# Feed-forward of a two-layer fp32 encoder step: another spread of the token scale, another order at its beginning, turn and end

## The reference, cut to what matters

```python
D_MODEL, D_FF, EPS = 1024, 4096, 1e-6

def rmsnorm(x, g):
    y = x * lax.rsqrt(jnp.mean(x * x, axis=-1, keepdims=True) + EPS)
    return y * g

def sq_relu_ffn(x, g, w1, w2):            # w1 (1024, 4096), w2 (4096, 1024), all float32
    h = jax.nn.relu(rmsnorm(x, g) @ w1)
    return (h * h) @ w2

for l in range(2):
    x = x + mixer[l](rmsnorm(x, norm_mix_g[l]))
    x = x + sq_relu_ffn(x, norm_ffn_g[l], w_ff1[l], w_ff2[l])
y = rmsnorm(x, norm_out_g)                # and the new caches and states
```

## Time and profile before

| | us |
|---|---|
| median of 3 runs (lowest, highest) | 2695.02 (2692.13, 2702.24) |
| the profiled execution | 2700.55 |
| its span, first to last instruction | 2698.6 |
| outside the span (the difference) | 1.95 |
| PE busy | 2607.2 (97%) |
| DVE, ACT, POOL busy | 1741.4, 957.2, 1499.1 |

### The profile page before, as it was taken

One profiled execution on the slowest core, in us unless ns is written; L12 is line 12 of the kernel. 1 busy time (PEld: TensorE's weight loads), 2 busy tenths in 40 slices (PEclk: granted clock), 3 DMA queues, 4 the chain that ended last, 5 costly groups with the idle time before them and its releaser, 6 DMA issues. The chain is left out here.

```text
span 2698.6 us, 44221 instructions
## 1 busy us (share of the span) xinstructions
PE 2607.2 (97%) x17409; PEld 2525.2 (94%) x17409; DVE 1741.4 (65%) x2291; ACT 957.2 (35%) x1828; POOL 1499.1 (56%) x1527
## 2 busy tenths in 40 slices
PE   7999999999998999999999999989999999899998
PEld 7998789999997999999989898979999999899997
DVE  5216956766666777778646464654766666777776
ACT  4112634333333434441413323142433333344444
POOL 6543523666665888873222321342466667688784
PEclk9999999999998999999999999999999999999999
DMA  6321021333345434432233241433133334534332
GB/s 196 71 55 42 2 113 66 119 141 140 140 149 196 152 138 141 140 130 74 37 98 42 76 83 55 97 115 131 50 139 140 140 140 178 199 135 144 136 134 95
DMA packets 161789, 308.21 MB, mean 114 GB/s; under 512 B 61628, under 2 KB 76988, under 8 KB 160816
## 3 DMA queue, kind: packets, MB, share of 16 engines
q1 hardware_dynamic: 86656, 243.19, 26.6%
q10 hardware_dynamic: 74656, 61.22, 7.8%
q0 software_dynamic: 272, 0.98, 0.1%
HBM read 204.18 MB, written 95.85 MB: 111 GB/s over the span
## 5 line engine op out<-in xcount | busy, mean ns | idle before, releaser
L741 POOL TENSOR_TENSOR w_lo<-w_raw,w_hi 128x256 fp32r<-128x256 f32 (+1 forms) x478 | 435.2, 923 | 267.4 <-ACT w_hi L2317 267.2
L1006 PE MATMUL psum<-a_hi,w_hi 128*128 128x288 f32 x2032 | 441.2, 299 | 12.1 <-DVE low L1760 11.7
L1760 DVE TENSOR_TENSOR low<-low,psum 128x576 f32<-128x576 f32 x441 | 330.7, 751 | 170.4 <-PE psum L1006 168.0
L1006 PE MATMUL psum<-a_lo,w_hi 128*128 128x288 f32 x2032 | 438.1, 298 | 0.0
L1006 PE MATMUL psum<-a_hi,w_lo 128*128 128x288 f32 x2032 | 437.8, 297 | 0.0
L2317 ACT ACTIVATE w_hi<-w_raw 128x256 fp32r<-128x256 f32 (+1 forms) x478 | 209.5, 456 | 537.8 <-POOL w_raw L755 305.0
L1006 PE MATMUL psum<-op_h,w_hi 128*128 128x288 f32 x2040 | 357.4, 297 | 16.3 <-DVE low L1760 13.8
L1006 PEld LDWEIGHTS psum<-a_hi,w_hi 128*128 128x128 f32 x2032 | 331.5, 191 | 14.4 <-DVE low L1760 12.7
L1006 PEld LDWEIGHTS psum<-a_lo,w_hi 128*128 128x128 f32 x2032 | 330.9, 191 | 0.0
L1006 PEld LDWEIGHTS psum<-a_hi,w_lo 128*128 128x128 f32 x2032 | 330.3, 190 | 0.0
L951 PE MATMUL psum<-a_hi,w_hi 128*128 128x384 f32 x1272 | 302.6, 346 | 17.8 <-DVE a_lo L1551 16.4
(11 more groups left out here) (314 smaller groups left out, 4623.9 us busy)
## 6 DMA issues: line engine op xcount, KB each, us to landing
w_raw<-in_wall SPq DMA_DIRECT2D x159, 512.0 KB, 4.5
ffn_rows<-low SPq DMA_DIRECT2D x224, 288.0 KB, 2.1
mid<-ffn_rows SPq DMA_DIRECT2D x52, 576.0 KB, 3.6
rbc<-ffn_rows SPq DMA_DIRECT2D x50, 576.0 KB, 3.7
mid<-in_wall SPq DMA_DIRECT2D x32, 512.0 KB, 4.5
low<-in_x ACTq DMA_DIRECT2D x16, 576.0 KB, 8.3
high<-in_mem_in ACTq DMA_DIRECT2D x32, 257.0 KB, 4.3
out_mem_s<-high ACTq DMA_DIRECT2D x32, 257.0 KB, 3.2
```

The costliest lines, as they stand in the source:

```text
L741: nc.gpsimd.tensor_tensor(w_lo_flat[:, at], src, w_hi_flat[:, at].bitcast(F32), ALU.subtract)\
L1006: r = mm(psum[:, bank + i, 0:QT], v[:, at.start + P * k:at.start + P * (k + 1)], rows(part, k)[:, qtok(i)], start=start and k == 0 and n == 0,
L1760: V.tensor_tensor(dst, dst, two(bank), ALU.add).then_inc(dn_read, 1)
```

## The change

It touches the three stretches of each feed-forward that were just described, and has three parts.

**First pair.** The diagonal on DVE goes. PE makes each half of the spread with six matmuls of 96 columns: the stationary operand is a column of `rstd12` repeated 128 times, the moving one the 96x96 identity. Both halves stand behind product 4. ACT loads its table for the root with a one-column Sqrt at the start of the feed-forward, and raises T3 later in its queue; DVE makes T1's low part ahead of the T4 difference, and has some low parts in another order.

**Turn.** Chunk 0's last row is staged in H0 instead of mid. DVE has the lowering of rows 4, 5, 6 of chunk 0 behind the adds 0, 2, 3 of unit 0, the last pair's last sum and ReLU behind add 4, and its other sums behind the products 6, 7, 8. SP reads rows (0,6) and (1,1) and the weights of unit 2 ahead of the last pair's last writes. Chunk 1's rows are raised and lowered at the products that two tables give: the raising at q = 10, 12, 16, 18, 22, 24, 27 (before: 5, 8, 11, ... 23), the lowering of one half each behind the adds 11 to 14, 17 to 20, 23 to 26, 28 and 29 (before: 7, 8, 10, 11, 13, 14, ... 25, 26).

**End.** `rest` and `add_squares` of the last chunk work on 576 columns in twice as many steps; in feed-forward 0 the rests of tiles 4 to 7 (before: 6 and 7) stand behind the last add.

```diff
+CHUNK0_AT = ("A", "A", "H0", "H1", "mid", "A", "H0")
+CHUNK1_HIGH = {10: 0, 12: 1, 16: 2, 18: 3, 22: 4, 24: 5, 27: 6}
+CHUNK1_LOW = {11: (0, 0), 12: (0, 1), 13: (1, 0), 14: (1, 1), 17: (2, 0), 18: (2, 1), 19: (3, 0), 20: (3, 1),
+              23: (4, 0), 24: (4, 1), 25: (5, 0), 26: (5, 1), 28: (6, 0), 29: (6, 1)}
...
-                per = {"A": 3, "mid": 26, "H0": 1, "H1": 1}[n]
+                per = {"A": 3, "mid": 25, "H0": 2, "H1": 1}[n]
...
                         sp.wait_ge(c_relu, 4 * PAIRS * (f + 1))
+                    elif q == 1:
+                        sp.wait_ge(d_lo, 14 * FC * f + 10)
                     else:
                         sp.wait_ge(d_lo, 14 * FC * f + 14 + 2 * (q - 1))
...
+                    if p == PAIRS - 1:
+                        sp.wait_ge(d_lo, 14 * FC * f + 6)
+                        rows_in(0, 6)
+                        next_rows(1, 1)
+                        sp.wait_ge(f_split, n0 + NPU + 7)
+                        down_load(2)
                     sp.wait_ge(t_out, 4 * n + 1)
                     keep(p, "T1")
                     if p == PAIRS - 1:
-                        sp.wait_ge(d_lo, 14 * FC * f + 10)
-                        rows_in(0, 6)
                         next_rows(1, 0)
-                        sp.wait_ge(f_split, n0 + NPU + 7)
-                        down_load(2)
                         sp.wait_ge(h_sq, 4 * n + 4)
                         keep(p, "B21")
...
-                for k in range(3):
-                    x_return(k)
+                x_return(0)
+                x_return(1)
                 for d in range(DUNITS):
                     c, j = divmod(d, 4)
-                    if d == 1:
+                    if d == 2:
+                        sp.wait_ge(t4_out, 16 * PAIRS * (f + 1))
+                        x_return(2)
                         sp.wait_ge(d_lo, 14 * FC * f + 12)
                         x_return(3)
                     if c + 1 < FC:
-                        for i in range(max(2 * j, d == 0), min(2 * j + 2, 7)):
+                        for i in range(2 if d == 0 else 2 * j, min(2 * j + 2, 7)):
...
-                    pe.wait_ge(diagonal, 2 * f + h + 1)
-                    if h:
-                        pe.wait_ge(rstd_copied, 2 * f + 1)
-                    for i in range(2):
-                        r = mm(psum[:, bank + i, 0:QT], ones[0:COLT, :], c21[0:COLT, qtok(i)], start=True, stop=True)
+                    pe.wait_ge(ff_sum, f + 1)
+                    for n in range(NC // 2):
+                        at = COLT * (n % 3)
+                        r = mm(psum[:, bank + n // 3, at:at + COLT],
+                               rstd12[0:COLT, NC // 2 * h + n:NC // 2 * h + n + 1].to_broadcast([COLT, P]),
+                               ident[0:COLT, 0:COLT], start=True, stop=True)
                     r.then_inc(rstd_done, 1)
...
                     product(Z, at, kt, rows, True, True, ready)
-                    if first:
-                        spread_scale(0, W)
                     at, kt, rows, ready = begin(4)
                     pe.wait_ge(up_read, r0 + 4 * p + 1)
                     product(X, at, kt, rows, False, False, ready)
                     if first:
-                        spread_scale(1, W)
+                        spread_scale(0, W)
+                        pe.wait_ge(up_read, r0 + 2)
+                        spread_scale(1, Z)
                     at, kt, rows, ready = begin(5)
                     product(V, at, kt, rows, True, True, ready)
                     at, kt, rows, ready = begin(6)
...
-                def scale_diagonal(h):
-
-                    n = NC // 2
-                    V.tensor_tensor(c21[0:COLT, :].rearrange("p (a b) -> p a b", a=n),
-                                    ident[0:COLT, 0:COLT].unsqueeze(1).to_broadcast([COLT, n, COLT]),
-                                    rstd12[0:COLT, n * h:n * (h + 1)].unsqueeze(2).to_broadcast([COLT, n, COLT]),
-                                    ALU.mult).then_inc(diagonal, 1)
-
...
-                        if d == 0 and i in (0, 2):
-                            rows_low(0, 5 + i // 2)
-                        if d == 0 and i in (4, 5, 6):
-                            late_sums(PAIRS - 1, i - 4)
-                        if c == 0 and q >= 7 and q % 3 != 0:
-                            rows_low(1, (q - 7) // 3, ((q - 7) % 3,))
-                        elif 0 < c < FC - 1 and q % 4 >= 2:
+                        if d == 0 and i in (0, 2, 3):
+                            rows_low(0, 4 + (i + 1) // 2)
+                        if d == 0 and i == 4:
+                            first_sum(PAIRS - 1)
+                            last_relu(PAIRS - 1)
+                        if d < 2 and 6 <= q <= 8:
+                            late_sums(PAIRS - 1, q - 6)
+                        if 28 * c + q in CHUNK1_LOW:
+                            at1, part = CHUNK1_LOW[28 * c + q]
+                            rows_low(1, at1, (part,))
...
-                                    rest(2, k + i - 4, KT + k + i - 4 + 1)
+                        if c == FC - 1 and q >= 7:
+                            if f == 1 and i in (1, 2, 4, 5):
+                                add_squares(4, 2 * (j - 1) + i // 4, ((i - 1) % 3,))
+                            elif f == 0 and 8 <= q < 24:
+                                half_step((q - 8) // 4, (q - 8) % 4)
+                            elif f == 0 and q >= 24:
+                                add_squares(2, 4 + (q - 24) // 2, (q % 2,))
+
+                def half_step(k, n):
+                    if n < 2:
+                        rest(2, k, KT + k + 1, parts=(n,))
+                    else:
+                        add_squares(2, k, (n - 2,))
 
...
+                    for k in range(KT - 4, KT):
                         rest(2, k, KT + k + 1)
+                    for k in range(KT - 2, KT):
                         add_squares(2, k)
...
+                A(table[:, :], ones[:, 0:1], ACT.Sqrt)
...
                     elif c == 1 and i == 0:
-                        act.wait_ge(d_lo, 14 * FC * f + 10)
+                        act.wait_ge(d_lo, 14 * FC * f + 14)
...
+                        if d == 0 and i == 3:
+                            squared(PAIRS - 1, 3)
+                        if c == 0 and q in CHUNK1_HIGH:
+                            rows_high(1, CHUNK1_HIGH[q])
```

More of the change, by code:

```diff
@@ L175, in build @@
         mats = sb("mats", [P, NK, P])
+        table = sb("table", [P, 1])
         head_par = sb("head_par", [P, NH])
@@ L1711, in up @@
                     if first:
[L1712 to L1716 removed]
+                        for k in range(1, 4):
+                            lowered("B22", k)
                     else:
@@ L1736, in up @@
                         rows_low(0, 3)
-                    dve.wait_ge(h_sq, sq + 3)
-                    t_sum(ct1, c12, c11)
-                    dve.wait_ge(f_done, done + 7)
-                    relu(c21, 0, two(X))
-                    if final:
-                        rows_low(0, 4)
-                    else:
-                        late_sums(p, 0)
-                        late_sums(p, 1)
+                        return
+                    first_sum(p)
+                    if first:
+                        dve.wait_ge(held, 64 * (f + 1))
+                    last_relu(p)
+                    late_sums(p, 0)
+                    late_sums(p, 1)
                 def down(d):
@@ L2408, in ffn @@
                     if first:
-                        late_operands()
+                        for k in range(4):
+                            scaled("T3", k, 1)
+                        raised("B22", 3)
                     else:
@@ L2419, in ffn @@
                     weights(n + 1)
+                    if first:
+                        late_operands()
                     weights(n + 2)
@@ L2424, in ffn @@
                     weights(n + 3)
+                    if final:
+                        weights(n + 4)
                     if first:
                         scale_out(0, W)
-                    if final:
-                        weights(n + 4)
-                    if not first:
-                        squared(p, 0)
+                        scale_out(1, Z)
+                    squared(p, 0)
                     if final:
```

99 lines of the change are left out of this document (41 added, 58 removed).

## The result

The kernel after took 2706.57 us (median of 20 runs, 2697.28 to 2710.59), the kernel before 2700.59 in 20 runs of the same series (2688.89 to 2705.64). The ratio is 1.0024, 95% interval 1.0014 to 1.0034: 6.5 us slower, between 3.8 and 9.2. The forecast was 7.0 us faster, and 2688 as the time. The profiled execution took 2704.41 us, span 2702.6.

What follows compares the result with a forecast made beforehand. PE bounds the kernel, busy 2607 of 2699 us, so only its idling or slow clock can give time. First pair -12.4, turn +8.1, end -2.7 sum to -7.0: 2688 from the runs' median of 2695.02, range 2660 to 2705.

Steps and rivals of the forecast that it cites:

- First pair, forecast -12.4: First pairs of both feed-forwards: idling, slow clock and operand waits go, less 2.9 per new spread; 12.4 us gained, 9.4 to 14.0.
- no clock should fall: First pairs: product 4 follows product 3 at once, so no wait is left and PE stays at full clock.
- The third rival: First pair's spread doesn't overlap or waits, 4.4 us or more apiece: 2691, inside the forecast; no separate chance given.
- Turn, forecast +8.1: Both turns: excess of 21.3 us each against 18.6 and 15.9 before; 8.1 us lost, from 2 gained to 24 lost.
- Both new stalls: Each turn, before products 20 and 26: late weights of units 3 and 4 stop PE 6.8 and 6.1 us, plus 2.2 clock each.
- units 0 and 1: Start of each turn: about 4 us of excess kept, 3 if one step hides, 7 if the first wait partly stays.
- The two rivals with fewer stalls: Turns: no new stalls, 2653, chance 0.10; or one stall in each turn, 2671, chance 0.10.
- the rival of late reads: Turns: weights' reads land late among other transfers, each us more counting in four chains, 12.6 us lost: 2701, chance 0.12.
- The upper end of the turn's range: Both turns: 24 us lost if units 0 and 1 keep 7 each and loads are as slow as row (1,1).
- End, forecast -2.7: Ends of both feed-forwards: halves go between adds, removing waits of 3.7 us, less 1; 2.7 gained, between nothing and 3.7.
- I count 1 us of it: End of feed-forward 0: of some 2.7 us more of DVE rests behind the last add, 1 us delays the next product.
- The rule against the halves: End: VectorE with two SBUF inputs and GpSimd share ports per instruction, so halves can wait for POOL; about 1 us gained.

Runs made afterwards that it cites:

- end_only: The kernel before with the end of the change alone, first pair and turn as before: 2703.61 us, ratio 1.0016 to the kernel before.
- end_order: The kernel before with halves at the end, squares of tiles 6 and 7 between the last rests, feed-forward 1's halves one product later: 2698.25 us, ratio 0.9998.
- table_only: The kernel before with only the one-column tile and the early Sqrt on it (table loaded ahead, later tiles shifted by 4 bytes): 2702.13 us, ratio 1.0004.

## Why the prediction was wrong

By the stages of the profiles, mean of three of after less mean of five of before: first pairs -10.5, turns +10.8, the ends +1.5 (+0.6 up to the gate product's tenth matmul behind the token sums in feed-forward 0, +0.9 from the last chunk of feed-forward 1 on), the attention +3.5, and all stages together +4.5 (the other stages -0.8). Timed alone, the parts are -7.6, +13 and +4.3, which sum to about +10 with wide intervals; the whole is +6.5. Each part alone was timed 2 to 5 us above its stages, and in each of the three profiles the attention ended 2.5 to 4.8 us later than the mean of before; that the runs without a profile lost the same there was not shown.

- **First pair, forecast -12.4.** The mechanism held: no diagonal, product 4 directly behind product 3 in feed-forward 0, spread 2.6. The size was short by 2 in the stages, and 1.6 of that is the clock: product 3 of feed-forward 0 ran at 0.64, where the forecast said that no clock should fall. A wait of 0.46 stayed in feed-forward 1, about what the spreads of 2.6 instead of 2.9 give back. The third rival, a spread of 4.4, falls.
- **Turn, forecast +8.1.** Both new stalls came in both feed-forwards, at the products named, behind the queue named. Waits and chain were right within 1.3 us each. The term was some 3 too small. 1.6 of this is the excess itself, 22.3 and 22.0 instead of 21.3 each: units 0 and 1 kept 5.0 and 6.1 instead of 4, while the stalls with their clock took 17.3 and 15.9, where 17.3 was counted. Another 0.6 is the baseline: against the mean of five executions of before the first turn of that profile was 1.3 us slow and the second 0.6 fast, and a forecast from one profile takes over its luck. The two rivals with fewer stalls and the rival of late reads fall. The upper end of the turn's range, 24 lost, is 27 by its own terms (8.1, 3 more for each turn's units 0 and 1, and 12.6 for late reads); nothing hangs on it.
- **End, forecast -2.7.** This is the step that failed: "I count 1 us of it". The forecast counted the rests of the last tiles as hidden beside the gate product, which uses these tiles last. The rests are indeed used last, but the squares of tiles 6 and 7 stand behind them on DVE, and the token sums that wait for the squares come ahead of the gate product's last two tiles. The forecast did not take the place of the sums in that product into account. PE waited 2.26 us there and lost clock behind the wait. In feed-forward 1, half an operation one product earlier meets ACT's square, which is not there yet. By the stages the end thus cost 1.5 in the kernel after and nothing in `end_only`, instead of gaining 2.7. `end_order` shows the order as the cause: same halves, no wait for squares, and 3.0 gained in its stages. The size that was forecast was in reach, and the order gave it away.
- **The rule against the halves** came from the Trainium skill, SBUF — State Buffer, section SBUF: two separate sides. The trace agrees with it as to the waits: of the 16 halves of squares that DVE added up in the kernel after four took 0.74 or 0.75 us, ten 0.86 to 1.33 and two 2.29 and 2.30, and each of the two longest ended 0.6 after an operation of POOL that was running when it began (the second is the one at 1211.24 above):

```profile
1206.72 2.29 DVE L1580 TENSOR_TENSOR mid<-mid,high 128x576 f32<-128x576 f32 x1
...
1205.61 2.79 POOL L740 TENSOR_TENSOR w_lo<-w_raw,w_hi 128x1024 fp32r<-128x1024 f32 x1
...
1210.13 2.79 POOL L740 TENSOR_TENSOR w_lo<-w_raw,w_hi 128x1024 fp32r<-128x1024 f32 x1
```

So a half lost about 1.5 us where the whole lost 2.0. The gain of about 1 at the end that the forecast drew from the rule is not what came: with the squares in the right order the ends gained 3.0.

Two more things lay outside the three parts. The forecast's base, the median of 3 runs, 2695.02, was 5.6 below the median of 20, so 2688 and the range around it lay that much too low by the luck of three runs. And the attention, for which the forecast had no term, ended 3.5 later; why stays open. By its own terms the sum, -7.0, lay near the line: in the stages the end missed by 4.2, the turn by 2.7 and the first pairs by 1.9, 8.8 together, which turns the sign without the attention.

## What to carry to other kernels

When an operand's step is put later in a table, follow the queue that its release opens: here a lowering moved three products later held a row's read, behind it the read of weights that had nothing to do with it, and four engines later the add that PE needed. Put a transfer that waits for nothing ahead of those that wait. When work is moved behind the last instruction of a loop, look for the first consumer of each moved piece, not of the tile they belong to. And take baselines from several executions, of a stage and of the whole: here one turn was slow by 1.3 us and the median of three runs low by 5.6, where 7 were looked for. In the other direction, a gain of 2 us that the times of whole kernels could not show stood clearly in a stage whose length hardly varies.

## What was not expected of the hardware

- In one execution (`table_only`), PE ran the pairs of feed-forward 1 faster at the same granted clock of 1.00: 387 records in 50 us where others have 377, that is 129 against 133 ns a record. From product 5 of the first pair to the turn it took 335.5 us, in the kernel before 343.1 to 344.4. The cause was not found. Window 2100 to 2150 of `table_only` and of the first profile of before:

```profile
2100.00:2150.00 50.00, 50.00 (x387) 1.00 0.38 143
```

```profile
2100.00:2150.00 50.00, 50.00 (x377) 1.00 0.37 138
```

- The issue of one write (out_v_s) held ACT for 1.87 and 1.88 us in two of three profiles of the kernel after and for 1.55 to 2.15 in five other kernels, but for 0.44 or 0.45 in all five profiles of before, in the third of after and in the other five kernels. It went with a late end of the attention each time, but late ends came without it too; what does it was not found.
